# An input projection in seven products for two tiles instead of eight

## The chip, the cores and the metric

One core of one Trainium2 chip runs the whole kernel. The engines are TensorE (PE in the rows, its weight loads PEld), VectorE (DVE), ScalarE (ACT), GpSimd (POOL) and SyncE (SP), which issues nearly all transfers. The metric is the device time in microseconds (us) of one execution.

## What is computed

One layer of a trunk, applied with the same weights to 128 context tokens and 1024 latent tokens. All numbers are float32. The part that the change touches is the modulated norm and the input projection:

```python
h = rmsnorm(x, norm1_g) * (1 + mod[:, 1]) + mod[:, 0]
p = (h @ w_in + b_in).astype(jnp.float32)      # h: (tokens, 1024), w_in: (1024, 2576)
q, k, v = heads(p[..., 0:512]), heads(p[..., 512:1024]), heads(p[..., 1024:1536])
o, gates, u = p[..., 1536:2048], p[..., 2048:2064], p[..., 2064:]
...
out = jnp.concatenate([hm, fu], axis=-1).astype(h.dtype) @ w_out   # hm: gated mLSTM of q, k, v; fu: DFT of u
x = x + mod[:, 2] * out
x = x + mod[:, 5] * expert_choice_moe(rmsnorm(x, norm2_g) * (1 + mod[:, 4]) + mod[:, 3])
```

The 16 gate columns give the logs of the input and forget gates, from which cumulative sums, running maxima and exponents over all 1152 tokens are formed (the forget-gate work below).

## The kernel before

The kernel has three parts that follow each other with a barrier between: `front` (modulation vectors and the input projection), `mixing` (mLSTM, DFT, output projection, router) and the experts. The change is in `front`. Every engine has its own instruction list, written out by hand; semaphores tie them together, and an engine takes its list in strict order.

The tokens are 9 tiles of 128: tile 0 is the context, tiles 1 to 8 the latents. `w_in` lies in SBUF as five blocks: q, k, v, o (512 columns each) and gates + Fourier (16 + 512). For a tile, SP loads x, ACT takes the mean of squares, GpSimd the power -0.5 (`invert_rms`), DVE scales (`normed`), PE transposes x into two PSUM banks `ps_x` (`turn_x`), DVE copies four of the eight 128x128 pieces with scale and shift into `hT`, ACT the other four (`keep_h`). Then PE takes, per block, eight contraction steps of 128 with 512 columns into one of two banks `ps_p` (`block_sum`, L483), and DVE adds the bias into `pr` (L657). [...] Between the blocks PE has the gate columns of the tile (`gate_sum`, L492, and `gate_join`, L498), transposes of q and k (`turn`, L507), and the column DFT of the tile before (`dft_cols`, L551). ACT copies q and k out, takes the sigmoid of o, and SP stores k, v, o and the transposed q, k to DRAM.

In tiles 0 and 1 PE also works through the modulation weights `ada_w` in 24 slices of 1 MB (`slice_sum`, L411), of which slices 10 to 23 stand inside tile 1, in runs of two and three. From slice 8 on they pass through four slots (`held`) in the area that later holds `w_out`. In the last tile DVE has the forget-gate work (`forget_start` to `forget_exponents`, L682 to L739), ACT its exponentials (L381), and PE four products that spread the gate rows (`spread_gate`, L425). After the last block come the transposes of the exponents (L573), the DFTs of tile 8 and one small product (L579), and then the barrier.

## Time and profile before

| | us |
|---|---|
| three runs, lowest, median, highest | 2220.86, 2221.1, 2221.1 |
| span of the profiled execution | 2218.4 |
| start to tile 1's first block | 72.1 |
| tiles 1 to 8 (to the last block's end, some 394.4) | 322 |
| rest of `front` | 6 |
| `mixing` and the experts | 1818 |

The span runs from the first to the last instruction of one execution under the profiler. The execution's own time is not noted apart from the runs; the table has their median beside the span. In the stretch of tiles 1 to 8 the five blocks of a tile are followed by the next tile's, with small PE work between.

### The profile page before, as it was taken

The numbers are of one execution on the slowest core, as the hardware profiler recorded it, in microseconds if no ns is written. First come the engines' busy times: TensorE is split into PE (matmuls) and PEld (weight loads), VectorE is DVE, ScalarE is ACT, GpSimd is POOL, SyncE is SP. The second block draws the span as 40 slices with busy tenths as digits, with TensorE's granted clock in tenths as the row PEclk, the third lists the DMA queues.
The fourth block names the chain that finished last, engine by engine and source line by source line (L and its number), as shares of the span: only waits on it lengthen the run. The fifth ranks groups of instructions, "written<-read, shape, count | busy, mean of one in ns | idle before, by whom it ended". The sixth has DMA issues, their size and how long they took to land.

```text
span 2218.4 us, 36881 instructions
## 1 busy us (share of the span) xinstructions
PE 2170.8 (98%) x15110; PEld 1860.6 (84%) x15110; DVE 492.5 (22%) x1262; ACT 359.4 (16%) x1029; POOL 255.9 (12%) x260
## 2 busy tenths in 40 slices
PE   7999999999978999999999999999999999999998
PEld 3444444865538999999999999999999999999996
DVE  1111116678872011100111011101111111001103
ACT  1111112433320111111111111101111011111103
POOL 0000000112111021020211202012020210202100
PEclk9999999999989999999999999999999999999999
DMA  9820100934475496977969689696986969769692
GB/s 382 330 105 33 66 33 24 319 135 157 136 258 174 162 360 214 367 214 261 332 224 367 211 292 295 233 364 211 323 259 239 361 212 354 226 249 347 220 382 95
DMA packets 352019, 528.19 MB, mean 238 GB/s; under 512 B 13933, under 2 KB 292573, under 8 KB 348777
## 3 DMA queue, kind: packets, MB, share of 16 engines
q1 hardware_dynamic: 337408, 509.24, 66.1%
q0 software_dynamic: 14336, 18.29, 3.9%
q8 instruction: 25, 0.41, 0.1%
q10 hardware_dynamic: 232, 0.11, 0.0%
q14 instruction: 18, 0.14, 0.0%
HBM read 492.23 MB, written 35.36 MB: 238 GB/s over the span
## 4 chain that ended last, share of the span: by engine, by line
PE 68%; DVE 1%; ACT 0%; issue 0%; DMA 0%; POOL 0%; DVEq 0%; ACTq 0%
PE ps_pair L1908 45%; PE ps_pair L1921 23%; DVE area L2100 0%; DVE area L2105 0%; PE ps_pair L1941 0%; DMA xe_p<-normed,slot_row_p 0%; ACT squares L1862 0%; PE ps_pair L1935 0%; POOL rs L1810 0%; DVE xeT L2034 0%; PE ps_pair L792 0%; PE ps_pair L1946 0%; DVE yS L2110 0%; ACT rs L1864 0%; PE ps_pair L1882 0%
## 5 line engine op out<-in xcount | busy, mean ns | idle before, releaser
L1908 PE MATMUL ps_pair<-xeT,area 128*128 128x144 f32 x8192 | 1006.2, 286 | 1.2 <-DVE xeT L2034 1.2
L1908 PEld LDWEIGHTS ps_pair<-xeT,area 128*128 128x128 f32 x8192 | 1004.6, 190 | 1.5 <-issue 1.5
L1921 PE MATMUL ps_pair<-hidT,area 128*128 128x144 f32 x4096 | 504.4, 286 | 0.0
L1921 PEld LDWEIGHTS ps_pair<-hidT,area 128*128 128x128 f32 x4096 | 502.8, 190 | 0.0
L483 PE MATMUL ps_p<-area,hT 128*128 128x512 f32 x720 | 317.4, 594 | 1.1 <-DMA area<-in_w_in 1.1
L2046 DVE TENSOR_TENSOR hidT<-silu,ps_pair 128x144 f32<-128x144 f32 x256 | 77.9, 304 | 881.3 <-ACT silu L1826 815.8
L483 PEld LDWEIGHTS ps_p<-area,hT 128*128 128x128 f32 x720 | 133.5, 190 | 154.7 <-issue 151.7
L1801 POOL DMA_INDIRECT stream<-ye,slot_row x60 | 94.7, 1578 | 1131.8 <-DVE ye_p L2057 1118.1
L1826 ACT ACTIVATE silu<-ps_pair 128x144 f32<-128x144 f32 x256 | 74.3, 290 | 907.4 <-PE ps_pair L1908 889.3
L1243 PE MATMUL b_z<-w_out,shared 128*128 128x512 f32 x288 | 128.7, 598 | 2.4 <-DVE soft L1591 1.7
L2050 DVE STREAM_TRANSPOSE yS<-yT 128x1024 f32<-128x1024 f32 x15 | 18.7, 1245 | 425.9 <-ACT yT_p L1833 425.9
L1832 ACT ACTIVATE yT<-ps_pair,mod 128x128 f32<-128x128 f32 x128 | 47.0, 367 | 390.0 <-PE ps_pair L1921 390.0
L1243 PEld LDWEIGHTS b_z<-w_out,shared 128*128 128x128 f32 x288 | 53.0, 190 | 64.5 <-issue 59.0
L657 DVE TENSOR_TENSOR pr<-ps_p,area 128x512 f32<-128x512 f32 x45 | 31.1, 691 | 270.9 <-PE ps_p L483 262.2
L1780 POOL DMA_INDIRECT xe<-normed,slot_row x60 | 58.1, 968 | 27.7 <-issue 22.9
L131 POOL TENSOR_TENSOR area<-area,minus_half 128x1 f32<-128x1 f32 x9 | 4.9, 550 | 312.1 <-ACT area L125 312.1
L1833 ACT ACTIVATE yT_p<-ps_pair,mod 128x16 f32<-128x16 f32 x128 | 34.1, 266 | 0.0
L1818 ACT ACTIVATE xeT<-xeS,mod 128x128 f32<-128x128 f32 x60 | 24.7, 482 | 22.9 <-DVE xeS L2022 22.9
L1070 ACT ACTIVATE area<-b_i,cols 128x129 f32<-128x129 f32 x72 | 20.5, 367 | 25.0 <-PE b_i L1222 17.5
L1803 POOL DMA_INDIRECT stream<-ye_p,slot_row_p x15 | 23.3, 1554 | 4.6 <-issue 4.6
L411 PE MATMUL ps_ada<-w_out,area 128*2 128x512 f32 x176 | 23.3, 662 | 0.5 <-DMA w_out<-in_ada_w 0.5
L123 ACT ACTIVATE squares<-x_area 128x1024 bf16<-128x1024 f32 x9 | 9.5, 1057 | 74.8 <-DMA x_area<-in_x_latent 74.7
(320 smaller groups left out, 1056.4 us busy)
## 6 DMA issues: line engine op xcount, KB each, us to landing
area<-in_exp_w SPq DMA_DIRECT2D x384, 1024.0 KB, 12.3
w_out<-in_ada_w SPq DMA_DIRECT2D x22, 1024.0 KB, 8.0
kvo<-pr SPq DMA_DIRECT2D x9, 768.0 KB, 3.3
area<-in_w_in SPq DMA_DIRECT2D x3, 2048.0 KB, 17.7
shared<-kvo SPq DMA_DIRECT2D x12, 512.0 KB, 5.5
qkT_dram<-qkT SPq DMA_DIRECT2D x9, 512.0 KB, 4.6
area<-qkT_dram SPq DMA_DIRECT2D x9, 512.0 KB, 5.9
area<-m_lanes SPq DMA_DIRECT2D x9, 512.0 KB, 6.8
```

Of the source, the lines that this page charges most:

```text
L483: mm = nc.tensor.matmul(ps_p[(par + b) % 2][:], hT[:, par, k], g.w_blocks[b][:, k, W_FROM[b]:W_FROM[b] + 512], start=(k == 0), stop=(k == ...
L657: g.dve.did(nc.vector.tensor_tensor(pr[:, par, b], ps_p[(par + b) % 2][:], g.b_in_row[:, COLS[b]:COLS[b] + 512], ALU.add), block_kept)
L1243: mm = nc.tensor.matmul(b_z[h][:], mixT[:, par, k], g.w_out_sb[:, k, bass.ts(h, 512)], start=(k == 0), stop=(k == DT - 1))
L1780: nc.gpsimd.indirect_dma_start(xe[:, c], None, normed_quarters, bass.IndirectOffsetOnAxis(ap=g.slot_row[:, c, e:e + 1], axis=0)).then_inc( ...
L1801: nc.gpsimd.indirect_dma_start(stream_quarters, bass.IndirectOffsetOnAxis(ap=g.slot_row[:, c, e:e + 1], axis=0), ye[:, c], None, compute_o ...
L1818: ins = nc.scalar.activation(xeT[:, k, 0:CAP_L].rearrange("p (s r) -> p s r", r=QUARTER), xeS[:, :, k], ACT.Identity, scale=g.mod[:, 1, 2, ...
L1826: nc.scalar.activation(silu[:, f % 2], ps_ab[f % 2][:, 0:N], ACT.Silu).then_inc(silu_ready, 1)
L1832: nc.scalar.activation(yT[:, d], ps_yy[d % 2][:, 0:CAP_L], ACT.Copy, scale=g.mod[:, 1, 4, d:d + 1])
L1833: nc.scalar.activation(yT_p[:, d % 4, d // 4], ps_yy[d % 2][:, CAP_L:N], ACT.Copy, scale=g.mod[:, 0, 4, d:d + 1]).then_inc(yT_kept, 1)
L1908: mm = nc.tensor.matmul(ps_ab[f % 2][:, N * w:N * w + N], unit[:, k, bass.ts(c, P)], xeT[:, k], start=(k == 0), stop=(k == DT - 1))
L1921: mm = nc.tensor.matmul(ps_yy[d % 2][:, 0:N], unit[:, f % 2, bass.ts(d, P)], hT[:, f], start=(f == 0), stop=(f == FT - 1))
L2046: nc.vector.tensor_tensor(hT[:, f], silu[:, f % 2], ps_ab[f % 2][:, N:2 * N], ALU.mult).then_inc(h_kept, 1)
```

## The change

Two latent tiles (a pair, `q` = 0 to 3, tiles 2q+1 and 2q+2) are projected together. Their `h` and a pair of weight blocks form a 2 x 2 by 2 x 2 product of quarters (two tiles by two halves of the contraction; two halves of the contraction by two column blocks), and the seven-product form of that (with 15 sums) takes the place of eight quarter products. A pair has three groups: q with k, v with o (512 columns per quarter), and the two halves of the Fourier block (256 columns). `n` counts the 12 groups. The products stand in the order P1, P2, P6, P5, P4, P7, P3; each is four contraction steps. P1, P6 and P7 add up in one bank, P2 and P4 use the other, P5 and P3 a bank `ps_mixed`. Per group DVE forms three weight sums (`first_sum`, `second_sum`, `third_sum`) in two former slots of the modulation slices, GpSimd the fourth; per pair DVE forms two sums of tokens (t1, t2), GpSimd two (t4, t3). The results are put together on DVE in seven steps, with one copy on ACT.

With it move: the slices pass through two slots instead of four, each at a place of its own (14 of them in groups 0 to 2); a tile's transposes are taken in halves through one bank, and ACT makes all copies into `hT`; the gate columns are taken for a pair at once; the forget-gate work is cut into pieces between the sums of the last pair; two of the gate-row products come in group 7 and two behind the last product, with their copies on ACT; ACT's three exponentials come behind the last product. The loop over tiles is written out. Tile 0 is projected as before.

```diff
-        slot_of = [0, 1, 2, 3, 4, 5, 0, 1] + [(n + 2) % HELD for n in range(SLICES - DT)]
+        slot_of = [0, 1, 2, 3, 4, 5, 0, 1, 2, 3] + [n % 2 for n in range(DT + 2, SLICES)]
...
+        h11, h21, h12, h22 = hT[:, 1, 0:KH], hT[:, 1, KH:DT], hT[:, 0, 0:KH], hT[:, 0, KH:DT]
+        t1, t2 = (g.gate1[:, 0, bass.ts(n, 512)].rearrange("p (k n) -> p k n", k=KH) for n in range(2))
+        t3, t4 = h12, g.side_b21[:]
+        sum_a, sum_b = (held[:, s].rearrange("p (k n) -> p k n", k=KH) for s in (2, 3))
...
+        P1, P2, P6, P5, P4, P7, P3 = range(7)
+        S0, C11, S1, S2, C22, C21, C12 = range(7)
...
+        def quarter(n, kh, nh):
+            ks = slice(KH * kh, KH * kh + KH)
+            if n % 3 == 2:
+                return g.w_blocks[4][:, ks, N_GATES + 256 * nh:N_GATES + 256 * nh + 256]
+            return g.w_blocks[2 * (n % 3) + nh][:, ks, 0:512]
...
+                def fourth_sum(n):
+                    cols = cols_of(n)
+                    pool.wait_ge(block_summed, summed(n, P6))
+                    TT(sum_b[:, :, 0:cols], quarter(n, 1, 0), sum_b[:, :, 0:cols], ALU.subtract).then_inc(pool_sums_set, 1)
+                def sides(q):
+                    pool.wait_ge(dve_sums_set, by_dve(q, "t2"))
+                    TT(t4, h21, t2, ALU.subtract).then_inc(pool_sums_set, 1)
+                    pool.wait_ge(parts_summed, q + 2)
+                    TT(t3, h22, h12, ALU.subtract).then_inc(pool_sums_set, 1)
...
+                def keep_half(q, h):
+                    par, ks = 1 - h // 2, KH * (h % 2)
+                    act.wait_ge(x_turned, 2 + 4 * q + h + 1)
+                    if q:
+                        act.wait_ge(block_summed, summed(3 * q - 1, (P1, P2, P7, P3)[h]))
+                    elif h >= 2:
+                        act.wait_ge(block_summed, 5)
+                        act.wait_ge(parts_summed, 1)
+                    for k in range(KH):
+                        g.act.did(nc.scalar.activation(hT[:, par, ks + k], ps_x[0][:, bass.ts(k, P)], ACT.Identity,
+                                                       scale=g.mod[:, 1, 0, ks + k:ks + k + 1], bias=g.mod[:, 1, 1, ks + k:ks + k + 1]), hT_ready_act)
...
+                def copy_corner(n):
...
+                    act.wait_ge(block_summed, summed(n, P5))
...
+                        act.wait_ge(y_summed, 4 * q + 2)
+                    g.act.did(nc.scalar.activation(result(n, 0, 1), ps_mixed[:, 0:cols_of(n)], ACT.Copy), corner_copied)
...
+                keep_y(TILES - 2, 0)
+                keep_spread(2, 0)
+                act.wait_ge(exponents_ready, 1)
+                g.act.did(nc.scalar.activation(wi_row, wi_row, ACT.Exp, scale=-1.0), weights_ready)
+                keep_y(TILES - 2, 1)
+                act.wait_ge(exponents_ready, 2)
+                g.act.did(nc.scalar.activation(em_row, em_row, ACT.Exp, scale=-1.0), weights_ready)
+                keep_y(TILES - 1, 0)
+                keep_spread(3, 1)
+                act.wait_ge(exponents_ready, 3)
+                g.act.did(nc.scalar.activation(t_row, t_row, ACT.Exp, scale=1.0), weights_ready)
+                keep_y(TILES - 1, 1)
...
+                def product(out, cols, tokens, weights, more=False):
+                    for k in range(KH):
+                        mm = nc.tensor.matmul(out[:, 0:cols], tokens[:, k], weights[:, k, 0:cols], start=(k == 0 and not more),
+                                              stop=(k == KH - 1), skip_group_check=True)
+                    mm.then_inc(block_summed, 1)
...
+                def group(n):
+                    q, gi = divmod(n, 3)
...
+                    chain, side = ps_p[(n + 1) % 2], ps_p[n % 2]
+                    if gi == 0:
+                        turn_half(q, 3)
+                        pe.wait_ge(hT_ready_act, half_ready(q, 0))
+                    pe.wait_ge(block_kept, kept(n - 1, C21) if n else 4)
+                    product(chain, cols, h11, quarter(n, 0, 0))
...
+                    if gi == 0:
+                        pe.wait_ge(hT_ready_act, half_ready(q, 1))
...
+                    product(side, cols, h21, quarter(n, 1, 0))
+                    if gi == 0:
+                        pe.wait_ge(hT_ready_act, half_ready(q, 3))
+                        gate_sum(q)
...
+                    if gi == 1:
...
+                        turn(2 * q + 1, 0)
+                    if gi == 2:
...
+                        if q < DUOS - 1:
+                            turn_half(q + 1, 1)
+                    pe.wait_ge(block_kept, kept(n, S0))
+                    pe.wait_ge(dve_sums_set, by_dve(q, "t2" if gi == 0 else f"s2_{gi}"))
+                    product(chain, cols, t2, sum_b, more=True)
...
+                    if n:
+                        pe.wait_ge(block_kept, kept(n - 1, C12))
+                    product(ps_mixed, cols, t1, sum_a)
...
+                    if gi == 0:
+                        gate_join(q)
...
+                    if gi == 2 and q < DUOS - 1:
+                        turn_half(q + 1, 2)
...
+                    pe.wait_ge(block_kept, kept(n, C11))
+                    if gi == 0:
+                        pe.wait_ge(pool_sums_set, by_pool(q, "t4"))
+                    product(side, cols, t4, quarter(n, 1, 1))
...
+                    if gi == 1:
+                        turn(2 * q + 2, 0)
+                    pe.wait_ge(block_kept, kept(n, S1))
+                    pe.wait_ge(dve_sums_set, by_dve(q, f"s3_{gi}"))
+                    if gi == 0:
+                        pe.wait_ge(pool_sums_set, by_pool(q, "t3"))
+                    product(chain, cols, t3, sum_a, more=True)
...
+                    if gi == 1:
+                        turn(2 * q + 2, 1)
+                    pe.wait_ge(corner_copied, n + 1)
+                    pe.wait_ge(pool_sums_set, by_pool(q, f"s4_{gi}"))
+                    product(ps_mixed, cols, h22, sum_b, more=True)
...
+                    if gi == 1 and q < DUOS - 1:
+                        turn_half(q + 1, 0)
...
+                def first_sum(n):
+                    cols = cols_of(n)
+                    if n:
+                        dve.wait_ge(block_summed, summed(n - 1, P7))
+                    else:
+                        dve.wait_ge(slice_used, DT + 1)
+                    did(TT(sum_a[:, :, 0:cols], quarter(n, 0, 1), quarter(n, 1, 1), ALU.add), dve_sums_set)
...
+                def second_sum(n):
+                    q, gi = divmod(n, 3)
...
+                    dve.wait_ge(dve_sums_set, by_dve(q, f"s1_{gi}"))
+                    if n:
+                        dve.wait_ge(block_summed, summed(n - 1, P3))
+                    else:
+                        dve.wait_ge(slice_used, DT + 2)
+                    did(TT(sum_b[:, :, 0:cols], sum_a[:, :, 0:cols], quarter(n, 0, 0), ALU.subtract), dve_sums_set)
...
+                def third_sum(n):
+                    cols = cols_of(n)
+                    dve.wait_ge(block_summed, summed(n, P5))
+                    did(TT(sum_a[:, :, 0:cols], quarter(n, 0, 0), quarter(n, 0, 1), ALU.subtract), dve_sums_set)
...
+                def last_corners(n):
...
+                    dve.wait_ge(block_summed, summed(n, P7))
+                    did(TT(result(n, 1, 1), ps_p[(n + 1) % 2][:, 0:cols], bias(n, 1), ALU.add), block_kept)
+                    dve.wait_ge(corner_copied, n + 1)
+                    dve.wait_ge(block_kept, kept(n, S2))
+                    did(TT(result(n, 0, 1), result(n, 0, 1), result(n, 1, 1), ALU.add), block_kept)
+                    dve.wait_ge(block_kept, kept(n, C22))
+                    did(TT(result(n, 1, 1), ps_p[n % 2][:, 0:cols], result(n, 1, 1), ALU.add), block_kept)
...
+                def mixed_corner(n):
+                    cols = cols_of(n)
+                    dve.wait_ge(block_summed, summed(n, P3))
+                    dve.wait_ge(block_kept, kept(n, S1))
+                    did(TT(result(n, 0, 0), ps_mixed[:, 0:cols], result(n, 0, 0), ALU.add), block_kept)
...
+                for q in range(DUOS):
+                    last = q == DUOS - 1
+                    for gi in range(3):
+                        n = 3 * q + gi
+                        first_sum(n)
+                        if last and gi == 1:
+                            forget_logs()
+                        if last and gi == 2:
+                            forget_last()
+                        if gi == 0:
+                            side_one(q)
+                        if n:
+                            mixed_corner(n - 1)
+                        if n == 1:
+                            dve.wait_ge(slice_used, 16)
+                            did(COPY(gate_rows_in, ps_ada[:]), row_kept)
+                        second_sum(n)
+                        if gi == 0:
+                            side_two(q)
+                        if last and gi == 1:
+                            forget_keep()
+                        start_chain(n)
+                        if n == 1:
+                            dve.wait_ge(mod_turned, 2)
+                            keep_shift(ps_qk[0], 3, 2)
+                        if n == 3:
+                            dve.wait_ge(slice_used, SLICES)
+                            did(COPY(turn_rows, ps_ada[:]), row_kept)
+                        if last and gi == 1:
+                            forget_sum(FWD)
+                        if last and gi == 2:
+                            forget_new()
+                        first_corner(n)
+                        if gi == 0:
+                            keep_parts(q)
+                        if gi == 1 and not last:
+                            normed(nc, g, dve, 2 * q + 3, 1, q + 1)
+                        if last and gi == 1:
+                            forget_sum(BWD)
+                        if last and gi == 2:
+                            forget_stable()
+                        second_chain(n)
+                        if last and gi == 1:
+                            forget_open()
+                        if last and gi == 2:
+                            forget_inter()
+                        third_sum(n)
+                        if gi == 0:
+                            keep_gates(q)
+                        if n == 3:
+                            dve.wait_ge(mod_turned, 3)
+                            keep_scale(ps_ada, 2, 0, 24)
+                            keep_shift(ps_ada, 4, 2)
+                        if gi == 1 and not last:
+                            normed(nc, g, dve, 2 * q + 4, 0, q + 2)
+                        if last and gi == 0:
+                            forget_start()
+                        if last and gi == 1:
+                            forget_peak(FWD)
+                            forget_peak(BWD)
+                        if last and gi == 2:
+                            forget_intra()
+                        last_corners(n)
+                mixed_corner(GROUPS - 1)
```

On PE, a tile's border in the loop before (L463 is the turning of x, `ps_x`; L483 a block; L492 and L498 the gate columns):

```order
L463 MATMUL ps_x0<-const,x_area 128x128 x4
L463 MATMUL ps_x1<-const,x_area 128x128 x4
L477 REGISTER_ALU
L483 MATMUL ps_p0<-area,hT 128x512 x8
L468 REGISTER_ALU
L489 REGISTER_ALU
L492 MATMUL ps_qk1<-hT,area 32x128 x8
L477 ISA
L483 MATMUL ps_p1<-area,hT 128x512 x8
L498 MATMUL ps_qk1<-area,const 128x128
```

And the first group of a later pair now (L583 turning of x, L649 a product, L642 the column DFT, L610 and L617 the gate columns of two tiles; `w_out` is where the weight sums lie, `gate1` t1 and t2, `side_b21` t4):

```order
L583 MATMUL ps_x0<-const,x_area 128x128 x4
L649 MATMUL ps_p0<-area,hT 128x512 x4
L642 MATMUL ps_y<-const,pr 128x128 x2
L649 MATMUL ps_p1<-area,hT 128x512 x4
L610 MATMUL ps_qk1<-hT,area 32x256 x8
L642 MATMUL ps_y<-const,pr 128x128 x2
L649 MATMUL ps_p0<-w_out,gate1 128x512 x4
L642 MATMUL ps_y<-const,pr 128x128 x2
L649 MATMUL ps_x1<-w_out,gate1 128x512 x4
L617 MATMUL ps_qk1<-area,const 128x256
L642 MATMUL ps_y<-const,pr 128x128 x2
L649 MATMUL ps_p1<-area,side_b21 128x512 x4
```

Blocks of eight steps have become products of four, whose operands are sums from DVE and GpSimd, and what stood between blocks stands between products.

On DVE, the last tile before, from its first block on (L657 adds the bias; L698 to L707 are forget-gate work):

```order
L657 TENSOR_TENSOR pr<-ps_p0,area 128x512
L594 SCALAR_TENSOR_TENSOR mod<-ps_ada,area 128x8 x2
L599 COPY mod<-ps_ada 128x8 x2
L698 SCALAR_TENSOR_TENSOR x_area<-x_area 64x1152
L700 SCALAR_TENSOR_TENSOR area<-pr,x_area 32x1152
L701 SCALAR_TENSOR_TENSOR area<-pr,x_area 32x1152
L703 TENSOR_SCALAR pr<-pr 64x1152
L657 TENSOR_TENSOR pr<-ps_p1,area 128x512
L626 COPY gate1<-ps_ada 128x512
L707 TENSOR_TENSOR area<-gate_rows,area 64x1152
L710 SCALAR_TENSOR_TENSOR area<-pr,area 32x1152
```

And the second group of the last pair now (L1015 to L1049 put results together, L1002 is the third weight sum; L894 to L904 are forget-gate work, scans printed as SCALAR_TENSOR_TENSOR):

```order
L1015 TENSOR_TENSOR pr<-ps_p1,area 128x512
L894 SCALAR_TENSOR_TENSOR area<-x_area 32x1152
L1022 TENSOR_TENSOR pr<-ps_p0,pr 128x512
L894 SCALAR_TENSOR_TENSOR area<-x_area 32x1152
L1035 TENSOR_TENSOR pr<-ps_p1,area 128x512
L898 TENSOR_SCALAR x_area<-x_area 64x1152
L899 TENSOR_TENSOR area<-gate_rows,area 64x1152
L1002 TENSOR_TENSOR w_out<-area 128x2048
L904 SCALAR_TENSOR_TENSOR area<-x_area,area 32x1152 x2
L1044 TENSOR_TENSOR pr<-ps_p1,area 128x512
L1047 TENSOR_TENSOR pr<-pr 128x512
L1049 TENSOR_TENSOR pr<-ps_p0,pr 128x512
```

The scans and the two operations before the maxima now stand ahead of the third weight sum, for which a product waits.

On ACT, the end of `front` before (L375 the sigmoid of o, L381 exponentials, L355 DFT copies):

```order
L375 ACT_TABLE_LOAD
L375 ACTIVATE pr<-pr 128x512
L381 ACT_TABLE_LOAD
L381 ACTIVATE x_area<-x_area 64x1152
L381 ACTIVATE area<-area 64x1152
```

And now (L447 the sigmoids, L459 the corner copy, L436 DFT copies, L465 gate rows, L527, L530 and L534 the exponentials):

```order
L459 ACTIVATE pr<-ps_x1 128x256
L436 ACTIVATE w_out<-ps_y 128x128x2
L465 ACTIVATE gate1<-ps_ada 128x512
L527 ACT_TABLE_LOAD
L527 ACTIVATE x_area<-x_area 64x1152
L436 ACTIVATE w_out<-ps_y 128x128x2
L530 ACTIVATE area<-area 64x1152
L436 ACTIVATE w_out<-ps_y 128x128x2
L465 ACTIVATE gate1<-ps_ada 128x512
L534 ACTIVATE x_area<-x_area 64x1152
L436 ACTIVATE w_out<-ps_y 128x128x2
```

The exponentials stand between copies that PE waits for, behind the last corner copy.

## Rows read from the trace of the kernel before

**Rows 1.** The page's first line.

```profile
span 2218.4 us, 36881 instructions
```

**Rows 2.** Busy time by stage: PE, PEld, DVE, ACT, POOL; granted clock, DMA share, GB/s.

```profile
0.00:72.00 72.00, 58.03 (x251) 23.45 (x251) 10.22 (x30) 10.07 (x20) 1.31 (x6) 1.00 1.00 391
72.00:162.80 90.80, 90.80 (x359) 39.80 (x352) 12.72 (x27) 11.08 (x24) 1.10 (x2) 1.00 0.51 189
162.80:352.70 189.90, 189.90 (x611) 91.42 (x610) 29.46 (x60) 27.78 (x61) 2.74 (x5) 1.00 0.13 46
352.70:394.40 41.70, 41.29 (x125) 18.48 (x124) 30.17 (x46) 12.05 (x13) 0.00 (x0) 1.00 0.09 33
```

**Rows 3.** Timeline of PE over one tile: start, duration, what, count.

```profile
162.84 0.65 PE L492 MATMUL ps_qk<-hT,area 128*32 128x128 f32 x16
...
171.05 7.03 PE L483 MATMUL ps_p<-area,hT 128*128 128x512 f32 x16
177.92 0.61 PE L551 MATMUL ps_y<-const,pr 128*128 128x128 f32 x4
178.36 0.60 PE L507 MATMUL ps_qk<-const,pr 128*128 128x128 f32 x4
...
200.81 0.65 PE L492 MATMUL ps_qk<-hT,area 128*32 128x128 f32 x16
```

**Rows 4.** Costliest groups of instructions: busy us, mean ns, idle before.

```profile
L1908 PE MATMUL ps_pair<-xeT,area 128*128 128x144 f32 x8192 | 1006.2, 286 | 1.2 <-DVE xeT L2034 1.2
```

**Rows 5.** Groups of DVE in the last tile.

```profile
L657 DVE TENSOR_TENSOR pr<-ps_p,area 128x512 f32<-128x512 f32 x6 | 4.1, 686 | 15.3 <-PE ps_p L483 15.3
...
L700 DVE TENSOR_TENSOR_SCAN area<-pr,x_area 32x1152 f32<-32x1152 f32 x1 | 2.5, 2546 | 0.0
...
L734 DVE TENSOR_TENSOR x_area<-area,x_area 64x1152 f32<-64x1152 f32 x1 | 1.4, 1351 | 0.0
```

**Rows 6.** Groups of POOL, over the whole span.

```profile
L1023 POOL TENSOR_TENSOR y_prompt<-shared,ss 128x1024 f32<-128x1024 f32 x9 | 17.1, 1903 | 9.4 <-DMA normed<-y_prompt 7.9 <-DVE shared L1538 1.0
...
L986 POOL TENSOR_TENSOR shared<-shared,cols 128x512 f32<-128x512 f32 x6 | 6.2, 1040 | 17.8 <-DMA shared<-kvo 14.8 <-PE b_i L1269 3.0
```

**Rows 7.** Timeline in `mixing`, and line L1597 alone: min/median/max ns.

```profile
483.39 1.89 POOL L1023 TENSOR_TENSOR y_prompt<-shared,ss 128x1024 f32<-128x1024 f32 x1
483.41 1.90 DVE L1597 SCALAR_TENSOR_TENSOR den<-area 128x8 f32<-128x8 f32 x1
...
L1597 DVE SCALAR_TENSOR_TENSOR den<-area x9: 171/1694/1899, 450.0 to 607.4; 128x8 f32<-128x8 f32 x9
```

**Rows 8.** Timeline of PE before tile 1, and ACT's copies of four pieces.

```profile
67.38 1.90 PE L411 MATMUL ps_ada<-w_out,area 128*2 128x512 f32 x16
69.10 0.62 PE L492 MATMUL ps_qk<-hT,area 128*32 128x128 f32 x16
...
71.49 0.64 PE L492 MATMUL ps_qk<-hT,area 128*32 128x128 f32 x16 [0.80 <-DVE gate_rows L639]
72.06 7.13 PE L483 MATMUL ps_p<-area,hT 128*128 128x512 f32 x16
...
60.02 1.49 ACT L342 ACTIVATE hT<-ps_x,mod 128x128 f32<-128x128 f32 x4
```

**Rows 9.** Timeline at the end of `front`, PE and then ACT.

```profile
387.36 7.13 PE L483 MATMUL ps_p<-area,hT 128*128 128x512 f32 x16
...
399.08 0.44 PE L579 MATMUL ps_ada<-x_area 64*128 64x72 f32 x2
400.33 0.45 PE L1193 MATMUL b_z<-const,w_out 128*128 128x256 f32 x1 [0.81 <-PEq L235]
...
387.86 1.28 ACT L381 ACT_TABLE_LOAD   x1
389.16 1.16 ACT L381 ACTIVATE x_area<-x_area 64x1152 f32<-64x1152 f32 x1
```

**Rows 10.** Slice loads (L244) from 60 to 120 us: issue to landing.

```profile
DMA to landing us min/median/max: 4.8/7.1/11.6
```

779 lines of the change are left out of this document (453 added, 326 removed).

## The prediction

> **What bounds the kernel now.** I read the stages first, then TensorE's (PE's) order of work inside one tile, then the engines beside it. The span is 2218.4 us [rows 1], and the times of three runs are 2221.1 us in the median, so some 2.7 us lie around the span. I make the sum against the span and carry the difference over. By stage [rows 2], PE is busy for 90.8 of 90.8 us, 189.9 of 189.9 and 41.3 of 41.7 in the three stretches that hold the latents' projection. VectorE (DVE) works 12.7, 29.5 and 30.2 us in them, DMA moves 189, 46 and 33 GB/s, and the granted clock is 1.00 of 2.4 GHz. So the projection is PE-bound, and an instruction taken from PE there is time gained, as long as nothing else comes late. One tile takes 200.81 - 162.84 = 37.97 us [rows 3], of which five blocks of 6.87 us (171.05 to 177.92) are 34.4. What follows from 400.3 on is started by the end of this stage and moves with it.
>
> **PE's work.** A block is 16 matmul rows of 512 columns: 429 ns each. A product of the new kind has half of the contraction, 8 such rows, 3.43 us. For 256 columns I need a price that this stage doesn't show: 144-column rows run back to back at 1006.2 / 8192 = 123 ns [rows 4], 0.85 ns a column, like the 512 ones at 0.84, so 256 columns take 215 ns and such a product 1.72 us. Bounds: the same by column, or no less than 123 ns a row by rows 4, which is far under it. Before: 8 tiles x 5 x 6.87 = 274.8 us. After: 4 pairs x (14 x 3.43 + 7 x 1.72) = 240.2. That removes **34.6 us**.
>
> Around it on PE: a gate sum is 0.57 us per tile (71.49 to 72.06, [rows 8]) and becomes one of double width per pair, which I take at 0.85 (0.57 to 1.14). With a step of 0.1 us for each change of matmul shape, the seven that lie behind 72.06 cost 7 x 0.67 = 4.7 and the four new ones 4 x 0.95 = 3.8: 0.9 saved. The modulation slices cost 0.86 each (67.38 to 69.10 is two, [rows 8]) and do so still, but stand alone at 14 places where they stood in 6 runs: 8 x 0.2 (a step in, a step out) = +1.6. The pair's first product starts later than tile 1's first block did (72.06): ScalarE (ACT) copies both halves of each tile through one bank, 1.49 us for four [rows 8], and PE waits once for the third copy before it can turn the fourth half, some 1.3 us. Since the gate sum of tile 1 isn't ahead of it any more, I get 72.4, +0.3; tile 2's turning (0.87, eight transposes, twice the four of 0.44 us in [rows 3]) is then behind us, -0.9. These sum to +0.1. Transposes, column DFTs and joins cost what they did.
>
> **Are the sums in time?** DVE needs, by [rows 5], 0.69 us for 512 elements from PSUM and 1.35 for 1152 with both inputs in SBUF, about 1.02 ns an element: 2.26 us for a weight sum of 2048, 1.2 for 1024. GpSimd (POOL) needs 1.90 for 1024 and 1.04 for 512 [rows 6], so 3.6 for 2048, 1.9 for 1024. The products stand as P1, P2, P6, P5, P4, P7, P3. In a 512-column group, with the end of P6 at 0:
> - POOL forms the fourth sum from 0.1 to 3.7. Its reader P3 is due at 10.3, so it has 6.6 us to spare.
> - P5 ends at 3.4 to 3.9 (with the transposes ahead of it). DVE's third sum then runs 3.9 to 6.2. P7 is due at 7.3 or later. In time by 1.
> - From the end of P7: three corners on DVE (2.1), first sum (2.3), mixed corner (0.7), second sum (2.3), start of the chain (0.7) end 8.3 after P7, and P6 of the next group is due at 3 x 3.43 = 10.3. In time by 2. With a pair's two side sums more (1.4) but the turning, the gate sum and DFTs in between, by 2 again.
> In a 256-column group the third sum has P4's 1.72 us alone, but a half tile's turning (0.43) stands there, except in the last pair: in time by about 0.1. The copies of the next pair's halves (1.5 + 0.2 us) meet products of 1.72: up to 0.1 late, twice a pair. I take **+0.5** for the first three pairs (0 to 3).
>
> **What DVE and POOL do to each other.** The one place where rows show it: while POOL's 1.89 us operation runs, a DVE operation on 128x8 started 0.02 us after it takes 1.90 us, though the shortest of its kind takes 0.171 [rows 7]. It ends with POOL's. So I price it as blocking, for DVE work with two SBUF inputs. That is also what the Trainium skill states (SBUF — State Buffer, Who interferes with whom): such a DVE instruction and a GpSimd one that reads SBUF exclude each other for the whole instruction, whichever came first; the trace agrees. The skill's GPSIMD Engine Reference (3.1 Elementwise) has 4497 ns for a two-input sum of 2048 elements, where my rows extrapolate to 3.6; by it a third sum would end 0.9 later and still before P7 in a full pair, and the total below would be some 1.3 us longer.
>
> In the first three pairs the blocking hides in the slack above. In **the last pair** it doesn't, because the forget-gate work (24 us of DVE time: four scans of 2.55, seven operations of 1.35, the rest small; until now under blocks of 6.87 us of which DVE had 0.69) is cut up between sums. I walked the second group of that pair, end of P7 of the group before at 0: three corners to 2.3, first sum 4.6, the logs 6.0, mixed corner 6.7, second sum 9.0, the memsets 10.3, chain start 11.0; PE could have begun P6 at 10.7, so 0.3 late. Then scan (2.55, [rows 5]) to 13.5, first corner 14.2, the second scan 16.8, which keeps POOL's fourth sum, ready at 14.6, from starting. POOL runs 16.8 to 20.4 and in turn holds up the two operations that open the peaks (to 22.5), so the third sum ends at 24.8, where P7 was due at 22.2: 2.6 late. The last group, the same way: P6 0.5 late (first sum, four copies, mixed corner, second sum), P7 2.6 late (two 1.35 us operations and POOL's 1.9 take turns ahead of the third sum). In all **+6.2 us**; without blocking the same walk gives 2.4.
>
> **The tail.** From the last block's end (387.36 + 6.97 = 394.3) to the next stage (400.3) it is 6.0 us [rows 9]: ACT had loaded its table (1.28) and taken three exponentials (1.16 each) under the last block. Afterwards they come behind the last product, between copies that PE's last DFTs wait for: copy, gate row, table, exponential, copy, exponential, copy, gate row, exponential, 7.6 us on ACT alone plus some eight hops of 0.2 between it and PE. I get 11.2 us: **+5.2**, of which 2.0 is PE work (two DFTs, one gate row) that leaves the body, **-2.0**. Loads of the next stage's first rows can start at the last corner and land within that tail.
>
> **Slices.** With two slots instead of four, a 1 MB slice is requested when the one two before it is used, and is needed after two products and a slice, 7.9 us later. In this stretch landings took 4.8 to 11.6 us, median 7.1 [rows 10], with three requested at once; alone I expect nearer 4.8. Cost 0 (up to 10 if each took the longest).
>
> **Sum**: -34.6 + 0.1 + 0.5 + 6.2 + 5.2 - 2.0 = -24.6 us on the span: 2193.8, and 2196.5 with the 2.7 around it. I say **2197**.
>
> **Rivals.**
> - As forecast, 2193 to 2201: chance 0.50.
> - DVE and POOL don't block each other for these shapes (rows 7 are one small operation), or the tail is shorter: last pair 2.4 instead of 6.2, so 2190 to 2193. Chance 0.17.
> - Sums come late in every group: the slack is 0.1 to 2 us, a DVE queue of some 16 operations a group is in strict order, and a hop costs 0.1 to 0.2. One us per group is +12: 2209 (2202 to 2213). Chance 0.20. For it speaks the thin slack of the 256-column groups, against it that most hops are already counted.
> - Slices starve the first pair: landings of 11.6 where 7.9 is given, on three or four: +5 to +10, 2202 to 2207. Against it: 189 GB/s in that stretch, where the first 72 us moved 391 [rows 2]. Chance 0.07.
> - Slower: POOL's fourth sum becomes the path. P3 waits for it, and the room is 10.3 us in a full group. Eight groups must lose 25 us, 3.1 each, so it decides from 13.4 us per sum, 3.7 times the row's price. A strided input of 4 x 512 and a second full operand are all that could do it: 2225. Chance 0.03, and 0.03 that losses just cancel.
>
> **The numbers.** 2197, range 2190 to 2209: it takes in the first two cases and most of the third and fourth; what is left out is about 0.15. A change within 0.2% (4.4 us) is what a measurement of this kernel can't tell from none. Faster 0.93, same 0.04, slower 0.03.
>
> **What the profile after would show.** Right: products at 3.43 and 1.72 us pitch, PE busy near 100% up to the last pair; weight sums of 2.3 on DVE and 3.6 on POOL; the third sum's wait behind POOL's end by 0.2 us in full groups; PE idle 2 to 3 us twice in the last pair with the sums on DVE as releaser; a tail of 11 us with ACT's exponentials in it. Wrong: PE idle before P7 or P6 in the first three pairs, a sum on POOL over 10 us, PE waiting for a slice, or a clock below 1.00 in the stage.

## The result, and the profile after

The changed kernel takes 2204.36 us in the median of four runs (2202.06 to 2205.08); the kernel before took 2221.1 in the same comparison (2220.86 to 2221.53, four runs). The ratio is 0.9923 (0.9911 to 0.9934): faster by 16.7 us, where 24 were forecast; inside the range, at 0.7 of the gain. The profiled execution has a span of 2203.0 us, 15.4 less than [rows 1], against -24.6 in the sum. The profiled execution took 2204.82 us, 1.8 more than its span. The prediction set 2.7 around the span of the kernel before, because it compared one execution's span with the median of others.

The page of the changed kernel, first its totals and then the granted clock by fortieths of the span (55 us each):

```profile
span 2203.0 us, 36810 instructions
PE 2147.6 (97%) x15070; PEld 1868.3 (85%) x15070; DVE 583.8 (27%) x1306; ACT 381.4 (17%) x1077; POOL 314.5 (14%) x280
PEclk9999998999979999999999999999999999999999
```

The same by stage, with the columns of [rows 2]: the first pair (groups 0 to 2), the second, the third, the last, and the tail.

```profile
72.80:157.00 84.20, 84.20 (x353) 38.40 (x352) 35.67 (x39) 15.06 (x33) 16.01 (x7) 1.00 0.59 205
157.00:225.00 68.00, 67.95 (x241) 37.78 (x240) 34.15 (x42) 15.44 (x35) 15.04 (x7) 1.00 0.14 54
225.00:295.00 70.00, 69.95 (x240) 37.70 (x240) 34.19 (x37) 16.65 (x37) 15.03 (x7) 1.00 0.12 46
295.00:367.40 72.40, 67.77 (x221) 36.53 (x220) 59.14 (x65) 14.38 (x22) 15.81 (x5) 0.98 0.10 37
367.40:380.80 13.40, 10.39 (x60) 7.50 (x58) 2.82 (x15) 7.16 (x11) 0.10 (x1) 0.71 0.52 159
```

PE is busy practically without a gap in three of four pairs, as forecast, and waits for no slice in the first. What matters is in the last two rows: in the last pair 4.6 us of PE's time are idle, DVE works 59 of 72 us, and the clock is no longer 1.00; in the tail it is 0.71. TensorE's order of work in the second group of the last pair (start, duration, and in brackets the idle time before it with its releaser):

```profile
330.07 3.70 PE L649 MATMUL ps_p<-w_out,gate 128*128 128x512 f32 x8 [0.19 <-DVE pr L1015]
337.48 3.60 PE L649 MATMUL ps_p<-area,side_b 128*128 128x512 f32 x8
340.92 0.60 PE L628 MATMUL ps_qk<-const,pr 128*128 128x128 f32 x4
344.30 5.37 PE L649 MATMUL ps_p<-w_out,hT 128*128 128x512 f32 x8 [2.78 <-DVE w_out L1002]
349.50 0.60 PE L628 MATMUL ps_qk<-const,pr 128*128 128x128 f32 x4
```

Two losses stand in the fourth row. The wait of 2.78 us was forecast (2.6). The duration was not: this product took 5.37 us, while its neighbours of the same shape take 3.60 to 3.70. VectorE and GpSimd in the same stretch:

```profile
333.22 2.55 DVE L894 TENSOR_TENSOR_SCAN area<-x_area 32x1152 f32<-32x1152 f32 x1
336.52 4.16 DVE L898 TENSOR_SCALAR x_area<-x_area 64x1152 f32<-64x1152 f32 x1
341.88 2.27 DVE L1002 TENSOR_TENSOR w_out<-area 128x2048 f32<-128x2048 f32 x1
333.86 6.21 POOL L384 TENSOR_TENSOR w_out<-area,w_out 128x2048 f32<-128x2048 f32 x1 [21.74 <-PE ps_p L649]
```

GpSimd's sum begins at 333.86 inside VectorE's scan and ends at 340.07, 4.3 us behind the scan's end (335.77); VectorE's operation issued at 336.52 ends 0.6 us behind GpSimd's. Undisturbed, GpSimd takes 4.52 us for 2048 elements. My extrapolation was 3.6, from operations whose second operand is broadcast (1.90 us for 1024 elements, [rows 6]); with two full operands 1024 elements take 2.36 us.

The tail, from the end of the last product (367.36) to the next stage:

```profile
367.36 0.61 PE L642 MATMUL ps_y<-const,pr 128*128 128x128 f32 x4
367.90 1.12 PE L564 MATMUL ps_ada<-small_area,const 64*128 64x512 f32 x2
369.59 0.75 PE L810 MATMUL ps_x<-const,area 36*128 36x36 f32 x9
372.54 0.75 PE L642 MATMUL ps_y<-const,pr 128*128 128x128 f32 x4 [2.20 <-ACT w_out L436]
373.22 1.17 PE L810 MATMUL ps_x<-const,x_area 36*128 36x36 f32 x9
374.21 2.05 PE L564 MATMUL ps_ada<-small_area,const 64*128 64x512 f32 x2
380.72 2.05 PE L1576 MATMUL b_z<-const,w_out 128*128 128x256 f32 x4 [0.81 <-PEq L269]
```

It takes 13.4 us (11.2 forecast, 6.0 in [rows 9]). PE waits 2.20 us for a copy that ScalarE does behind its table load and an exponential; behind the wait two gate rows of the same shape take 2.05 us where such a pair took 1.12 at 367.90: the lower clock.

The next stage begins 19.6 us earlier than in [rows 9] (380.72 for 400.33), yet the span is only 15.4 shorter: 4.2 us are lost in code that the change doesn't touch.

### The profile page after: what moved, and what is told of

Its sections match the earlier page's. It is cut to its first block, busy times and chain, and to the rows that moved or that the text cites. A ratio compares the mean times of both kernels' runs of the same rounds, so it can differ in the third digit from the quotient of the medians.

```text
span 2203.0 us, 36810 instructions
## 1 busy us (share of the span) xinstructions
PE 2147.6 (97%) x15070; PEld 1868.3 (85%) x15070; DVE 583.8 (27%) x1306; ACT 381.4 (17%) x1077; POOL 314.5 (14%) x280
## 4 chain that ended last, share of the span: by engine, by line
PE 69%; DVE 1%; issue 0%; ACT 0%; DMA 0%; POOL 0%; DVEq 0%; ACTq 0%
PE ps_pair L2292 46%; PE ps_pair L2305 23%; DVE area L2484 0%; DVE area L2489 0%; DMA xe_p<-normed,slot_row_p 0%; PE ps_pair L2325 0%; ACT squares L2246 0%; PE ps_pair L2319 0%; POOL rs L2194 0%; PE ps_pair L1175 0%; DVE xeT L2418 0%; PE ps_pair L2330 0%; DVE yS L2494 0%; ACT rs L2248 0%; PE ps_pair L2266 0%
## 5 line engine op out<-in xcount | busy, mean ns | idle before, releaser
L649 PE MATMUL ps_p<-area,hT 128*128 128x512 f32 (+1 forms) x192 | 71.9, 522 | 0.0
L384 POOL TENSOR_TENSOR w_out<-area,w_out 128x2048 f32<-128x2048 f32 (+1 forms) x12 | 47.5, 3954 | 170.3 <-PE ps_p L649 170.3
L649 PEld LDWEIGHTS ps_p<-area,hT 128*128 128x128 f32 x192 | 35.5, 190 | 28.9 <-issue 26.6
L649 PE MATMUL ps_p<-w_out,hT 128*128 128x512 f32 (+1 forms) x96 | 38.3, 543 | 4.4 <-DVE w_out L1002 4.4
L597 PE MATMUL ps_p<-area,hT 128*128 128x512 f32 x80 | 35.3, 593 | 1.5 <-DMA area<-in_w_in 1.5
L649 PE MATMUL ps_p<-w_out,gate 128*128 128x512 f32 (+1 forms) x96 | 36.5, 522 | 0.2 <-DVE pr L1015 0.2
L649 PE MATMUL ps_p<-area,side_b 128*128 128x512 f32 (+1 forms) x96 | 36.6, 523 | 0.0
L649 PE MATMUL ps_x<-w_out,hT 128*128 128x512 f32 (+1 forms) x96 | 36.4, 522 | 0.0
L649 PE MATMUL ps_x<-w_out,gate 128*128 128x512 f32 (+1 forms) x96 | 36.3, 521 | 0.0
L1002 DVE TENSOR_TENSOR w_out<-area 128x2048 f32<-128x2048 f32 (+1 forms) x12 | 29.0, 2419 | 25.1 <-PE ps_x L649 25.1
```

What stands on the lines that cost most here:

```text
L384: TT(sum_b[:, :, 0:cols], quarter(n, 1, 0), sum_b[:, :, 0:cols], ALU.subtract).then_inc(pool_sums_set, 1)
L597: mm = nc.tensor.matmul(ps_p[b % 2][:], hT[:, 0, k], g.w_blocks[b][:, k, W_FROM[b]:W_FROM[b] + 512], start=(k == 0), stop=(k == DT - 1))
L649: mm = nc.tensor.matmul(out[:, 0:cols], tokens[:, k], weights[:, k, 0:cols], start=(k == 0 and not more), stop=(k == KH - 1), skip_group_c ...
L1002: did(TT(sum_a[:, :, 0:cols], quarter(n, 0, 0), quarter(n, 0, 1), ALU.subtract), dve_sums_set)
```

## The experiments

All edits are against the changed kernel (2204.36 us). e1 to e4 ran together, then e5 to e8, then e9 to e11, each set with runs of the kernel before, which had medians of 2221.28, 2221.15 and 2220.09 us. The last set is 1.0 us lower, so 1.0 of its differences to the changed kernel (whose set had 2221.1) is the set's. Theory A: the exclusion of VectorE and GpSimd makes the waits of the last pair, and idle times of 2 to 3 us on TensorE cost as much again since the clock falls behind them.

**e1, third sum ahead of the forget pieces.**

```
+                        third_sum(n)
                         if last and gi == 1:
                             forget_open()
                         if last and gi == 2:
                             forget_inter()
-                        third_sum(n)
```

> In the last pair VectorE forms the third sum ahead of the two operations that open the peaks (group 10) and ahead of the first exponent (group 11), not behind them. Theory A (VectorE and GpSimd exclude each other, and the wait of 2.78 us is what lowers the clock for the product behind it): in group 10 the third sum still has to let GpSimd's sum end (340.07), so it ends near 342.3 and P7 begins near 342.4, 1.0 late where it was 2.8; in group 11 it is 0.4 late where it was 1.66. That is 3.0 us, and 1.8 more if the short wait leaves the clock at 1.00: 3.0 to 4.8 us less than the changed kernel. Rival B (no exclusion; VectorE's queue is only in a bad order): no wait before P7 in either group, so 4.4 to 6.2 less. Rival C (what stands in the queue elsewhere moves the wait to the last corners): the gain of P7 comes back at P6 of group 11, total within 1 us of the changed kernel.

Measured 2201.29 us (2200.67 to 2202.63), 3.1 less. PE's rows:

```profile
342.28 3.67 PE L649 MATMUL ps_p<-w_out,hT 128*128 128x512 f32 x8 [0.86 <-DVE w_out L1002]
351.65 3.72 PE L649 MATMUL ps_p<-area,hT 128*128 128x256 f32 x16 [1.82 <-DVE pr L1049]
362.18 1.97 PE L649 MATMUL ps_p<-w_out,hT 128*128 128x256 f32 x8 [1.16 <-DVE w_out L1002]
```

The wait before P7 fell to 0.86 (1.0 said), the product keeps 3.67 us; the third sum itself shows as 4.54 us on VectorE (issued 337.59, with GpSimd's sum ending at 339.98), where it takes 2.27 alone, so B is out. But the scans now keep the last corners, and P1 of group 11 waits 1.82: that is C's mechanism at half its size. In the profiled execution 1.7 us are gone at the end of the last product (365.70 for 367.36) and 2.2 at the end of the span.

**e2, PE kept awake in the wait.**

```
+                    if n >= GROUPS - 2:
+                        stay_awake(nc, g, ps_y, 4, 6 if n == GROUPS - 2 else 3)
                     pe.wait_ge(block_kept, kept(n, S1))
```

> TensorE does six fillers of 512 columns (0.43 us each) into a free bank while it waits before P7 of group 10, and three in group 11; no other engine's work changes. Theory A (P7 of group 10 took 5.37 instead of 3.60 us since the clock was lowered by the idle time): P7 takes 3.60, begins at the same time, total 1.8 us less, and if the fall of the clock in the tail has the same origin up to 2 more. Rival B (P7 was slowed by what VectorE did beside it, two scans from 344.19 to 349.3): P7 stays at 5.4, total the same within 0.5 us.

```profile
341.42 5.32 PE L1177 MATMUL ps_y<-const 128*128 128x512 f32 x12
346.57 3.60 PE L649 MATMUL ps_p<-w_out,hT 128*128 128x512 f32 x8
```

A filler matmul of 512 columns is two rows in the trace, not one, so the six took 5.2 us, twice what I priced, and P7 begins 2.3 later. It takes 3.60 us, with the same two scans beside it for most of that time (344.26 to 349.39): the slow product was the clock, and B is out. The 2.20 us wait in the tail is still there, and so are the slow rows behind it, so the fall in the tail has its own origin. The kernel is at 2202.06 us (2201.01 to 2202.94), though its next stage begins 1.6 later than the changed kernel's (382.29); the rest of the program is 3.5 shorter: 0.8 of that up to the experts' entry, 2.7 from there on. I come back to that below.

**e3, the exponentials ahead of the tail's copies.** ScalarE does the three exponentials, then keep_y and keep_spread in their old order.

```
+                act.wait_ge(exponents_ready, 1)
+                g.act.did(nc.scalar.activation(wi_row, wi_row, ACT.Exp, scale=-1.0), weights_ready)
+                act.wait_ge(exponents_ready, 2)
+                g.act.did(nc.scalar.activation(em_row, em_row, ACT.Exp, scale=-1.0), weights_ready)
+                act.wait_ge(exponents_ready, 3)
+                g.act.did(nc.scalar.activation(t_row, t_row, ACT.Exp, scale=1.0), weights_ready)
                 keep_y(TILES - 2, 0)
                 keep_spread(2, 0)
-                act.wait_ge(exponents_ready, 1)
-                g.act.did(nc.scalar.activation(wi_row, wi_row, ACT.Exp, scale=-1.0), weights_ready)
                 keep_y(TILES - 2, 1)
-                act.wait_ge(exponents_ready, 2)
-                g.act.did(nc.scalar.activation(em_row, em_row, ACT.Exp, scale=-1.0), weights_ready)
                 keep_y(TILES - 1, 0)
                 keep_spread(3, 1)
-                act.wait_ge(exponents_ready, 3)
-                g.act.did(nc.scalar.activation(t_row, t_row, ACT.Exp, scale=1.0), weights_ready)
```

> ScalarE takes its table and the three exponentials before the copies of the last DFTs instead of between them, as soon as VectorE has each exponent ready (362.6, 365.1, 366.7). Theory A (the tail of 13.4 us is made by the exponentials between the copies, and by TensorE's low clock after its 2.20 us of idle there): exponentials end at 368, the tail is 8 to 8.5 us, and with the clock up the next stage's first 10 us give 1.5 to 2 more: 5 to 7 us less than the changed kernel. Rival B (the tail is bound by the copies and by VectorE's columns, the exponentials hide): tail 12 us, 1 to 2 less. Rival C (the first copy now waits for the third exponential, which VectorE readies late): tail as long as before, total the same.

Measured 2197.88 us (2196.36 to 2199.07), 6.5 less. ScalarE's last exponential and PE's first row of the next stage:

```profile
366.43 1.16 ACT L529 ACTIVATE x_area<-x_area 64x1152 f32<-64x1152 f32 x1 [0.49 <-DVE x_area L943]
375.18 2.04 PE L1576 MATMUL b_z<-const,w_out 128*128 128x256 f32 x4 [0.81 <-PEq L269]
```

With the last product's end at 367.03, the tail is 8.15 us, and no row in it is slow. A holds, B and C don't.

**e4, one fourth sum moved to VectorE.**

```
-                    for n in (3 * q + 1, 3 * q + 2):
-                        fourth_sum(n)
+                        if n != GROUPS - 2:
+                            fourth_sum(n)
...
                         third_sum(n)
+                        if n == GROUPS - 2:
+                            TT(sum_b, quarter(n, 1, 0), sum_b, ALU.subtract).then_inc(pool_sums_set, 1)
```

> Only the fourth sum of group 10 is moved from GpSimd to VectorE, right behind the third: VectorE gets 2.27 us more work in the most crowded group, GpSimd does nothing there. Theory A (the exclusion between the two engines makes the wait): the operation that opens the peaks falls from 4.16 to 0.7 us, the third sum ends near 340.9 and P7 (due at 341.5) doesn't wait, nor does P3 (due 345, fourth sum ready at 343.1); with the clock up P7 is 3.6: 4.6 us less than the changed kernel. Rival B (VectorE has too much to do in the last pair, whoever forms the fourth sum): the wait before P7 stays at 2.8 and P3 or the last corners come later by 2.3: 0 to 2.5 us more.

VectorE's rows, then PE's:

```profile
336.67 0.75 DVE L899 TENSOR_SCALAR x_area<-x_area 64x1152 f32<-64x1152 f32 x1
338.61 2.28 DVE L1003 TENSOR_TENSOR w_out<-area 128x2048 f32<-128x2048 f32 x1
340.82 2.28 DVE L1142 TENSOR_TENSOR w_out<-area,w_out 128x2048 f32<-128x2048 f32 x1
```

```profile
341.51 3.60 PE L650 MATMUL ps_p<-w_out,hT 128*128 128x512 f32 x8
350.44 3.72 PE L650 MATMUL ps_p<-area,hT 128*128 128x256 f32 x16 [1.46 <-DVE pr L1050]
362.23 3.15 PE L650 MATMUL ps_p<-w_out,hT 128*128 128x256 f32 x8 [2.42 <-DVE w_out L1003]
365.17 2.44 PE L650 MATMUL ps_x<-w_out,hT 128*128 128x256 f32 x8
```

The operation that took 4.16 us takes 0.75 once GpSimd has nothing to do, at the same place in the queue; P7 waits for nothing, with more work on VectorE. So the exclusion is shown to be the cause of that wait. The total is 2204.68 us (2202.86 to 2205.01), no gain: P1 of group 11 now waits 1.46 us, its P7 2.42 instead of 1.66, and the clock falls there (3.15 and 2.44 us for products of 1.89). A named the mechanism of this wait; on the total it was wrong, and B, by which VectorE has too much to do in the last pair, was right.

**e5, GpSimd's sum twice.** 

```
+                    if n < GROUPS - 3:
+                        TT(sum_b[:, :, 0:cols], quarter(n, 1, 0), sum_b[:, :, 0:cols], ALU.subtract).then_inc(minus_half_set, 1)
+                        pool.wait_ge(minus_half_set, n + 3)
```

> GpSimd forms the fourth sum twice in the first nine groups (the second pass works on the first one's result, so that operand of P3 is wrong there); nothing else changes. One pass takes 4.5 us for 2048 elements and 2.4 for 1024. Theory A (a VectorE sum and a GpSimd sum exclude each other for the whole instruction): GpSimd holds from 0.1 to 9.2 us behind the end of P6, the third sum (ready at 3.9) runs from 9.2 to 11.5 where P7 was due at 7.4 to 8.3: 3 to 4 us late in five full groups, 2 in the first (slices stand between its products) and 2 in each 256-column group, 24 to 28 us in all, and where such an idle time lowers the clock up to 1.8 each more: 24 to 42 us slower than the changed kernel. Rival B (they run side by side): P3 is due 10.7 or later behind P6 and GpSimd is done by 9.2, so nothing waits: within 2 us of the changed kernel.

Measured 2204.55 us (two runs), no change; P6 of group 10 begins at 330.46, 0.4 later than in the changed kernel. GpSimd and VectorE in group 4:

```profile
195.71 4.52 POOL L385 TENSOR_TENSOR w_out<-area,w_out 128x2048 f32<-128x2048 f32 x1 [14.16 <-PE ps_p L652]
200.31 6.44 POOL L387 TENSOR_TENSOR w_out<-area,w_out 128x2048 f32<-128x2048 f32 x1
199.54 2.83 DVE L1005 TENSOR_TENSOR w_out<-area 128x2048 f32<-128x2048 f32 x1 [3.11 <-PE ps_x L652]
202.30 5.00 DVE L123 TENSOR_SCALAR x_area<-x_area,area 128x1024 f32<-128x1024 f32 x1
```

The forecast of A missed by 24 us, and the total is the one that B gave, but not because the engines run side by side. The exclusion is by instruction: VectorE's waiting sum slipped in between the two passes (it ends at 202.4; in the changed kernel at 202.5), GpSimd's second pass shows 6.44 us for 4.5, and VectorE's next operation 5.00 for 0.74. That last one is the normalising of a tile for the next pair, which nobody waits for yet. Here the second instruction didn't lengthen the hold on the waiting sum, and this run doesn't test what a longer hold would cost.

**e6, PE kept awake in the tail.**

```
                 turn_rows_of(0, e_row)
+                pe.wait_ge(block_kept, kept(GROUPS - 1, C12))
+                stay_awake(nc, g, ps_p[0], 4, 2)
                 dft_cols(TILES - 1, 0)
```

> Four filler rows of 512 columns (1.7 us) fill most of TensorE's wait of 2.20 us in the tail (370.3 to 372.5). Theory A (that wait lowers the clock to its lower level until about 385): the rows behind it take their full-clock times, which is 2.9 us less up to the next stage and 1 to 1.5 in its first 10 us: 3 to 4.5 us less than the changed kernel, and where the experts' first rows then meet a full clock up to 2.7 more. Rival B (the clock is lowered by the whole stretch's small rows, not by that wait): no gain, same within 0.5 us.

```profile
373.62 1.10 PE L564 MATMUL ps_ada<-small_area,const 64*128 64x512 f32 x2
378.27 2.04 PE L1578 MATMUL b_z<-const,w_out 128*128 128x256 f32 x4 [0.81 <-PEq L269]
```

2200.45 us (2199.90 to 2201.92), 3.9 less, with work added and none removed. The tail is 378.27 - 367.24 = 11.0 us, close to the 11.2 that I had forecast: what I had left out was the clock. The next stage's first 10 us have a mean clock of 0.83, as in the kernel before, where the changed kernel has 0.70.

**e7, last pair and tail in another order.** The fourth sums of groups 10 and 11 on VectorE; ScalarE's first exponential ahead of the tail's copies, the third ahead of keep_spread(3, 1); forget_peak(BWD) leaves group 10, and group 11 is:

```
+                def last_group(n):
+                    first_sum(n)
+                    mixed_corner(n - 1)
+                    second_sum(n)
+                    start_chain(n)
+                    forget_peak(BWD)
+                    first_corner(n)
+                    forget_last()
+                    second_chain(n)
+                    third_sum(n)
+                    late_fourth(n)
+                    forget_new()
+                    forget_stable()
+                    forget_inter()
+                    last_corners(n)
+                    mixed_corner(n)
+                    forget_intra()
```

> Last pair and tail put in another order: the fourth sums of groups 10 and 11 on VectorE; the backward peak scan into group 11 behind the start of its chain; in group 11 third and fourth sum ahead of the stabilisers, the last corners ahead of the two later exponents; ScalarE takes the first exponential before the tail's copies and the third before the last gate row's copy. Theory A: no wait over 0.5 us before a product of groups 10 and 11 (4.4 us less), no fall of the clock there (1.8), the last product ends near 361, the exponentials end near 368 and the next stage begins near 370 instead of 380.7: 8 to 11 us less than the changed kernel, some 2194 us, and 2191 if the experts' first rows meet a full clock. Rival B (VectorE's total in the last pair is the bound whatever the order): the waits only move, 2 to 4 us less, from the tail alone.

Measured 2195.87 us (2194.69 to 2196.82), 8.5 less, as A had it. No product of groups 10 and 11 waits over 0.2 us; the last ends at 360.42 instead of 367.36. The tail is 13.0 us, and behind a wait of 1.35 us in it the rows are slow again (e9 fills that wait):

```profile
363.43 0.68 PE L643 MATMUL ps_y<-const,pr 128*128 128x128 f32 x4 [1.35 <-ACT w_out L437]
366.92 2.05 PE L565 MATMUL ps_ada<-small_area,const 64*128 64x512 f32 x2
373.43 2.04 PE L1594 MATMUL b_z<-const,w_out 128*128 128x256 f32 x4 [0.81 <-PEq L269]
```

**e8, all twelve fourth sums on VectorE.** The edit of e4 for every n, behind a wait for GpSimd's side sum where gi is 0.

> VectorE forms all twelve fourth sums, right behind the third; GpSimd keeps only the two side sums of a pair. VectorE gets 8 x 2.27 + 4 x 1.2 = 23 us more. Theory A (since the two exclude each other, GpSimd's 4.5 us cost VectorE as much time as its own 2.27 would): in a full group third and fourth sum run 3.9 to 8.4 behind P6, P3 is due at 10.7, so the first three pairs cost the same within 1 us, and the last pair as in the run that moved one sum: within 2 us of the changed kernel, rather less. Rival B (VectorE is near its bound and GpSimd's work runs beside it for free): 1 us per group and more, 10 to 20 us slower.

2200.07 us (2198.98 to 2201.33), 4.3 less, more than A's 2, and B is out. P6 of group 10 begins at 330.14 (330.07 in the changed kernel), so nine groups cost nothing with 17 us more VectorE work (6 x 2.28 and 3 x 1.2); the gain is in the last pair, whose last product ends at 363.95 instead of 367.36. Third and fourth sum in group 4:

```profile
199.77 2.29 DVE L999 TENSOR_TENSOR w_out<-area 128x2048 f32<-128x2048 f32 x1 [3.11 <-PE ps_x L646]
201.98 2.28 DVE L1140 TENSOR_TENSOR w_out<-area,w_out 128x2048 f32<-128x2048 f32 x1
```

GpSimd's fourth sums buy nothing here: while GpSimd takes its 4.5 us, VectorE can't form a sum either.

**e9, e10, e11, fillers on top.** e9 is e7 with four filler rows in the wait of the tail; e10 is e9 with four more ahead of the experts; e11 is the changed kernel with these latter alone.

```
                 spread_gate(2, 0)
+                pe.wait_ge(qk_kept, 2 * TILES)
+                stay_awake(nc, g, ps_qk[0], 3, 2)
                 dft_cols(TILES - 2, 1)
...
                         mm.then_inc(slots_turned, 1)
+                stay_awake(nc, g, ps_at[0], 3, 2)
                 pe.wait_ge(h_kept, 2)
```

> The reordered last pair and tail (run e7_best, 2195.9 us), and in its tail four filler rows of 384 columns (1.3 us) in TensorE's wait of 1.35 us behind the first spread gate row. Theory A (a wait of that length lowers the clock for some 12 us; each idle stretch costs more than its length): the tail shrinks from 13.0 to 10 us, the next stage's first 10 us give 1.3 back, so 3 to 4.5 us less than e7_best, near 2192. Rival B (the tail of that run is bound by the exponentials on ScalarE and VectorE, whose last is ready at 367.7): only 1 to 2 less.

> As e9_best_tail, with four more filler rows of 384 columns behind the 64 transposes ahead of the experts, where TensorE idles for 2.3 us and the clock falls in the kernels with a late end. Theory A (what the changed kernel gives back at the experts' entry, 1.0 us of wait and 1.7 us of slow rows, comes of that idle time): 1.7 to 2.7 less than e9_best_tail, near 2190. Rival B (the fall there follows from where the entry lies against the clock's own rhythm, whatever is in the wait): 0 to 0.5 more than e9_best_tail.

> The changed kernel with the four filler rows ahead of the experts alone. Theory A as in e10_best_all: 1.7 to 2.7 less than the changed kernel (2204.4), with the rows at the experts' entry at full clock. Rival B: the same within 0.5 us.

e9: 2191.27 us (2190.79 to 2193.33), ratio 0.9872 (0.9857 to 0.9887): 4.6 less than e7 and 13.1 less than the changed kernel as measured, 3.5 and 12.1 if each is taken against the kernel before in its own set. With e10 it is the fastest version that was run. Its rows in the tail:

```profile
362.55 1.56 PE L1195 MATMUL ps_qk<-const 128*128 128x384 f32 x4
366.48 1.10 PE L565 MATMUL ps_ada<-small_area,const 64*128 64x512 f32 x2
370.50 1.98 PE L1596 MATMUL b_z<-const,w_out 128*128 128x256 f32 x4 [0.81 <-PEq L269]
```

Its tail is 370.50 - 360.96 = 9.5 us.

e10 takes 2191.36 us (2190.89 to 2192.49), the same as e9. It doesn't decide between A and B: in e9 TensorE waits only 1.36 us ahead of the experts' first rows and meets them at full clock, so there was nothing left for the filler to give back.

e11 takes 2203.28 us (2201.81 to 2203.91), 1.1 less than the changed kernel as measured and no less against the kernel before in its own set (16.8 us, the changed kernel 16.7). Its profiled execution has what A says of the rows: the wait ahead of the experts is 0.33 us instead of 2.27, and the clock behind it is 1.00. A's 1.7 to 2.7 us don't show in the median, so the size stays open.

## Why the forecast was right in its signs and 9 us off in its sum

Spans, forecast -24.6, measured -15.4; 1.3 us of the difference lies in which executions were profiled, since the medians differ by 16.7. The 9.2 by my own terms:

| term | forecast | measured |
|---|---|---|
| first product | 72.40 | 72.78 (0.4 late) |
| PE's work from first to last product, without the waits and the clock of the last pair | 286.0 | 288.2 (2.2 more) |
| waits in the last pair | 6.2 | 0.19 + 2.78 + 1.66 = 4.6 (1.6 less) |
| clock in the last pair | 0 | 5.37 - 3.60 = 1.8 |
| tail | 11.2 | 13.4 (2.2 more) |
| from the next stage on | as before | 4.2 more |

(286.0 is 394.33 - 72.06 = 322.27 with the terms -34.6, -0.9, +1.6, -0.9, +0.5 and -2.0; 288.2 is 367.36 - 72.78 = 294.58 less 4.6 and 1.8.)

**Products.** Right: 7.03 for two of 512 columns, 1.89 for one of 256, at pitches of 3.43 to 3.44 and 1.72 to 1.73 us. The second pair:

```profile
184.86 7.03 PE L649 MATMUL ps_p<-area,hT 128*128 128x512 f32 x16
216.93 1.89 PE L649 MATMUL ps_x<-w_out,gate 128*128 128x256 f32 x8
222.56 1.89 PE L649 MATMUL ps_x<-w_out,hT 128*128 128x256 f32 x8
224.47 0.63 PE L583 MATMUL ps_x<-const,x_area 128*128 128x128 f32 x4
```

What stands around them was priced 2.2 us too low, in six small terms that the rows show. At the end of the second and of the third pair a turning waits twice for ScalarE's copy, 0.2 each time (222.56 + 1.72 = 224.28, begun at 224.47): 0.8 where I had 0.5. The products, at pitches of 3.434 and 1.727 us, take 240.7 us where my rounded prices gave 240.2. The four gate sums of double width take 3.9 us where 0.85 each gave 3.4. The slices of tile 1 had stood in five runs and not six, which is one more step in and out (0.2). The two DFTs and the gate row took 1.7 us with them, not 2.0. And three waits of the last pair are 0.16 longer by pitch than the idle time shown, 0.5 together.

**The sums are in time** in the first three pairs: right, and the rival that had them late in every group is out. So are the two others that the profile can settle: no product waits for a slice (PE is busy for 84.20 of 84.20 us in the first pair), and no sum on GpSimd comes near 13.4 us. The third sum does wait behind GpSimd's in full groups, by 0.6 us (2.84 for 2.27 in group 4) where I had 0.2; P7 doesn't notice. e8 and e5 show more room than I gave them: 17 us more on VectorE, or a second pass on GpSimd, cost at most 0.4. GpSimd's own price was low by 0.9 (4.52 for 3.6). Here the Trainium skill (GPSIMD Engine Reference, 3.1 Elementwise) was the better source, with 4497 ns; the trace agrees. The 1.3 us on the total that I had worked out from it can't be seen: the two waits before P7 came to 4.4 us where I had 5.2.

**The exclusion** of the two engines: right, and shown by e4. For operations with two inputs in SBUF the trace agrees with the exclusion for the whole instruction that the Trainium skill (SBUF — State Buffer, Who interferes with whom) states: the third sum takes 4.54 us in e1, until 2.2 us behind the end of GpSimd's, and 2.27 alone. But my condition was too narrow. The operation that falls from 4.16 to 0.75 us in e4 is a `tensor_scalar` with one input in SBUF, and so is the one of 5.00 us in e5. An operation that reads PSUM wasn't held: L1035 in the changed kernel takes its usual 0.69 us at 335.80, within GpSimd's sum.

The walk through group 10 was right in its steps: from the end of P7 of group 9 (318.98), the second scan ends at 16.8 (16.8 forecast), GpSimd at 21.1 (20.4) and the third sum at 25.2 (24.8), with P7 due at 22.5 (22.2), hence 2.78 us late for 2.6. In group 11 the place was right and the size wasn't, 1.66 for 2.6. P6 was late by 0.19 and 0, where I had 0.3 and 0.5. The four waits of the walk add up to 6.0; the 6.2 in the sum is a slip.

**The tail** failed in one step: "7.6 us on ACT alone plus some eight hops of 0.2" counts PE's rows at full clock. With the clock held (e6) the tail is 11.0 us for my 11.2. That match is in part luck: the terms that I named come to 7.6 + 8 x 0.2 = 9.2 us, and the prediction doesn't say where the other 2.0 come from.

**The step that failed** behind most of this is the price of an idle TensorE. I listed "a clock below 1.00 in the stage" as a sign of error and gave it no price. I forecast PE idle for 2.6 us behind 270 us almost without a gap, and took the idle time as the whole cost. The runs show more: 1.8 us in the product behind it (gone in e2 with the wait filled, and in e1, e4 and e7 with the wait under 1 us), 2.3 in the tail (e6), and some 1.3 in the next stage's first 10 us (clock 0.70 for 0.83). The other step that failed is "What follows from 400.3 on is started by the end of this stage and moves with it": it came 4.2 us short of that. The wait's length alone doesn't decide it: waits of 1.66 us (P7 of group 11) and 1.82 (P1 in e1) were followed by rows at full clock, one of 1.35 between the small rows of e7's tail by slow ones.

**The give-back.** From the start of the next stage to the end, the kernel before has 2218.4 - 400.33 = 1818.1 us, the changed one 1822.3. About 1.5 are in that stage, whose first 10 us run at a clock of 0.70 instead of 0.83 (e6, e3 and e9 have 0.83 or 0.84 again). The other 2.7 are at the experts' entry 285 us later, where the changed kernel waits 2.27 us instead of 1.22 and its rows run more slowly. The experts and what follows, from their first row on, take one of two sizes in the profiled executions: 1537.8 to 1538.1 us in the changed kernel, e1 and e3 to e8, and 1536.1 to 1536.2 in the kernel before, e2, e9, e10 and e11, with nothing between. The size goes with the wait ahead of that first row. In the first group TensorE waits 1.89 to 2.43 us there, and the granted clock of the next 15 us is 0.89; in the second it waits 0.27 to 1.36 us, and the clock is 1.00. The 15 us behind the first row in the changed kernel and in e9, columns as in [rows 2]:

```profile
665.21:680.21 15.00, 15.00 (x109) 15.00 (x110) 0.92 (x3) 0.87 (x3) 3.64 (x4) 0.89 0.42 124
653.26:668.26 15.00, 14.99 (x122) 15.00 (x123) 0.91 (x3) 1.26 (x4) 4.26 (x5) 1.00 0.54 164
```

A clock of 0.89 for 15 us costs the 1.7 us between the sizes. So this looks like the same loss as in the last pair, a wait and the slow rows behind it, in code that the change doesn't touch. e11 bears it out: with the wait filled its rows are at full clock and it takes the small size. Why the kernel before, e2 and e9 have the short wait without a filler is open. Each kernel has one profiled execution, so it is open too whether this makes the executions of one kernel differ as they do (2202.06 to 2205.08 for the changed one). Gains of 1 us between two kernels here mean nothing for that reason.

## What to carry to other kernels

- Where a sum is handed to GpSimd to unload VectorE, price it as VectorE time too, at GpSimd's duration, for every VectorE operation that has both inputs in SBUF, and for a `tensor_scalar` with one (e4, e5). Here two engines sharing the four sums were no faster than VectorE alone, and slower where VectorE was crowded (e8).
- A cut of TensorE work in a stage that was bound by it makes the side work the bound at the stage's end, where it has no next tile to hide under. Walk the last pass and the tail row by row, and count for idle times of TensorE not only their length but the slower rows behind them; then look whether a reorder or a filler takes them away (12 to 13 us here, where the change itself gave 17).
- A wait that is taken away from a full queue comes back at the next reader (e1, e4), until the whole order is changed (e7).

## What was unexpected in the hardware

- The exclusion alternates by instruction: GpSimd 4.52, VectorE, GpSimd 6.44, VectorE 5.00 us (e5). An operation that is kept waiting shows as a long busy one, not as idle time.
- Filler work on TensorE made the kernel faster: 1.7 us of it took 3.9 us off (e6). It pays only where a wait is followed by slow rows; ahead of the experts in e10, where the rows were fast already, it gave nothing.
- The lower of the clock's two levels is seen in single rows: two gate rows of 512 columns 2.05 us for 1.12, nine 36-column transposes 1.17 for 0.75.
